# Feed-forward token groups of 384, 448 and 256, with one 512-column product for both halves of the last group

## The chip, the cores and the metric

One core of a Trainium2 chip runs the whole program. The metric is the device time of one launch in microseconds (us), as the median of three runs. TensorE (PE) does the matmuls, into eight PSUM banks of 512 fp32 columns; VectorE (DVE), ScalarE (ACT) and GpSimd (POOL) work elementwise; SyncE (SP) issues the DMAs. Each has its own instruction queue, and they wait for each other by semaphores.

## The reference

One inference step of one decoder layer, for 1024 prompt tokens and 8 x 8 sample tokens, 1088 in all, of width 1024:

```
def swiglu_ffn(x, g, w_gate, w_up, w_down):
    h = rmsnorm(x, g)
    return (jax.nn.silu(h @ w_gate) * (h @ w_up)) @ w_down

x = x + 0.5 * swiglu_ffn(x, ffn1...)                 # 1024 -> 2816 -> 1024
x = x + token_mixer(rmsnorm(x, mix_norm), ...)       # RG-LRU and GLA heads
x = x + cross_attend(x, mem_k, mem_v, ...)
x = x + 0.5 * swiglu_ffn(x, ffn2...)
y = rmsnorm(x, final_norm)
```

The change concerns the two feed-forward blocks, the norms before them and the final norm.

## The kernel before

The activations x lie in SBUF as [128, 8, 1088]: channels on partitions, 8 tiles of channels, tokens in the free dimension. Tokens go in three groups, `NS = [384, 384, 320]`; `tokens(n)` is the slice of group n. The same groups serve the feed-forward blocks and the mix.

**Products.** Every fp32 operand is split in a high part (rounded to the type fp32r) and a low part, the rest. `split_mm` (L1734 to L1738) makes a product of three matmuls: w_hi by x_hi, w_hi by x_lo, w_lo by x_hi, all accumulated in one PSUM bank.

**The feed-forward loop.** `ffn(f)` exists on each engine, for f = 0 and 1. It runs over 11 iterations of two tiles (ft) of the hidden width. The first and the last iteration are written out, nine run in a loop. An iteration on TensorE has six gate/up steps s, one for each ft and group n (in the first iteration the order is n slow, ft fast, so that both steps of group 2 come last; otherwise ft slow), each of 2 x 8 weight tiles, into banks 4 to 7 in two pairs (gate, up). Then come the down products: for each group n eight output tiles m, each of 2 weight tiles, into banks m % 4. Tile m waits until the addition three places back is done (`x_added`, the line `pe.wait_ge(x_added, ... + m - 3)`), so a bank is free again when TensorE returns to it.

**Behind a gate/up step**: ScalarE's silu from PSUM (L849); VectorE's product with the up bank (L1296, hf), its cast to h_hi (L1300) and the rest h_lo (L1302). **Behind a down tile**: VectorE adds half the bank to x (L1310). VectorE works strictly in order: the six steps' work, then the 24 additions.

**The weights**: per iteration SyncE loads six tiles of 512 KB each when the step that used the old ones is done (two after step 4 of 6, or 5 in the first iteration, two after step 6, two after the down products); ScalarE casts each (L772), GpSimd subtracts (L696). In the first feed-forward the same engines also split 60 tiles of the mix's weights for later (ScalarE L783, GpSimd L701).

**Norms** (rmsnorm) of a group: squares on ScalarE (L810), sums on VectorE (L1144, L1145) or GpSimd (L730, L732), column sums and spreading over the partitions by small matmuls (L1763, L1785), root on ScalarE (L823), scaling by VectorE (L1215, from x and a PSUM bank into frow), a_hi by ScalarE (L838), a_lo by VectorE (L1227). The norms of ffn groups 1 and 2 are made beside the first iteration's steps. In the last iteration of the first feed-forward VectorE makes the mix's first norm in between the additions of group 2; in the last of the second it makes rows of y (L1244) there, and then the remaining rows and their stores.

## Time and profile before

| | |
|---|---|
| median of 3 runs | 2378.79 us (2378.36 to 2382.55) |
| span of the profiled execution | 2379.0 us |
| TensorE busy | 2343.7 us, 99% |
| VectorE, ScalarE, GpSimd busy | 45%, 21%, 22% |
| TensorE's mean granted clock | 0.995 of full speed |
| first feed-forward, about | 8 to 811 us |
| mix and cross attention, about | 811 to 1568 us |
| second feed-forward and end, about | 1568 to 2379 us |
| a middle iteration of a feed-forward | 71.1 us |

The profile is of one execution; times in it are counted from the span's start. The recorded lengths of matmuls overlap, so what a matmul costs is read from the distance between starts. A bracket behind a row of the timeline gives the idle time of the engine before it and what ended it.

### The profile page before, as it was taken

How to read it: one execution, taken by the hardware profiler on the slowest of the kernel's cores; microseconds unless marked ns; L12 is line 12 of the kernel's file. 1: busy time of each engine (PE TensorE's matmuls, PEld its weight loads, DVE VectorE, ACT ScalarE, POOL GpSimd, SP SyncE). 2: the span in 40 equal slices, each digit the busy share in tenths (PEclk: the TensorE clock that was granted, in tenths of full speed). 3: DMA queues.
4: the chain of work that ended last, by engine and by line, in shares of the span. 5: the costliest groups of instructions: out<-in, count | busy, mean ns of one | idle time of the engine just before them, and what ended most of it. 6: DMA issues, size and time to landing. Idle time of an engine off the chain costs nothing. (4 is left out here: it accounts for less than half of the span.)

```text
span 2379.0 us, 36652 instructions
## 1 busy us (share of the span) xinstructions
PE 2343.7 (99%) x14996; PEld 2285.3 (96%) x14996; DVE 1062.5 (45%) x1696; ACT 494.6 (21%) x697; POOL 519.1 (22%) x239
## 2 busy tenths in 40 slices
PE   7999999999999999999999999999999999999998
PEld 7999999999999989899889999799999999999998
DVE  6434334444334574565642423444443344443345
ACT  4222212122211241321410221331111011111101
POOL 2444334344432000000001000022221222221121
PEclk9999999999999999999999999999999999999999
DMA  4554454454452465666678376731101010111112
GB/s 158 213 212 168 159 194 175 151 212 168 159 194 89 156 214 182 212 222 240 231 261 316 145 254 252 276 110 54 53 36 53 35 53 35 53 35 53 35 36 76
DMA packets 89475, 352.50 MB, mean 148 GB/s; under 512 B 8944, under 2 KB 16432, under 8 KB 79152
## 3 DMA queue, kind: packets, MB, share of 16 engines
q1 hardware_dynamic: 89104, 351.12, 40.3%
q8 instruction: 64, 1.05, 0.2%
q10 hardware_dynamic: 288, 0.18, 0.0%
q14 instruction: 19, 0.16, 0.0%
HBM read 280.54 MB, written 70.72 MB: 148 GB/s over the span
## 5 line engine op out<-in xcount | busy, mean ns | idle before, releaser
L1736 PE MATMUL ps<-a_hi,w_sb 128*128 128x384 f32 (+1 forms) x2112 | 691.6, 327 | 6.6 <-DVE a_lo L1227 4.6
L1738 PE MATMUL ps<-a_hi,w_sb 128*128 128x384 f32 (+1 forms) x2112 | 689.9, 327 | 0.0
L1737 PE MATMUL ps<-a_lo,w_sb 128*128 128x384 f32 (+1 forms) x2112 | 689.7, 327 | 0.0
L696 POOL TENSOR_TENSOR w_sb<-w_raw,w_sb 128x1024 fp32r<-128x1024 f32 x132 | 317.7, 2415 | 1066.4 <-ACT w_sb L772 1066.4
L1736 PEld LDWEIGHTS ps<-a_hi,w_sb 128*128 128x128 f32 x2112 | 397.7, 188 | 8.3 <-issue 3.5
L1737 PEld LDWEIGHTS ps<-a_lo,w_sb 128*128 128x128 f32 x2112 | 397.8, 188 | 0.0
L1738 PEld LDWEIGHTS ps<-a_hi,w_sb 128*128 128x128 f32 x2112 | 397.6, 188 | 0.0
L1310 DVE SCALAR_TENSOR_TENSOR x<-ps,x 128x384 f32<-128x384 f32 (+1 forms) x528 | 279.2, 534 | 199.7 <-PE ps L1738 199.7
L1296 DVE TENSOR_TENSOR hf<-sil,ps 128x384 f32<-128x384 f32 x132 | 70.1, 531 | 646.9 <-ACT sil L849 646.9
L1736 PE MATMUL ps<-h_hi,w_sb 128*128 128x384 f32 (+1 forms) x1056 | 344.7, 326 | 0.0
L1738 PE MATMUL ps<-h_hi,w_sb 128*128 128x384 f32 (+1 forms) x1056 | 344.2, 326 | 0.0
L1737 PE MATMUL ps<-h_lo,w_sb 128*128 128x384 f32 (+1 forms) x1056 | 344.1, 326 | 0.0
L849 ACT ACTIVATE sil<-ps 128x384 f32<-128x384 f32 x132 | 62.4, 473 | 1125.8 <-PE ps L1738 1125.7
L1302 DVE TENSOR_TENSOR h_lo<-hf,h_hi 128x384 fp32r<-128x384 f32 x132 | 239.5, 1815 | 4.6
L1736 PEld LDWEIGHTS ps<-h_hi,w_sb 128*128 128x128 f32 x1056 | 198.3, 188 | 0.3 <-DVE x L1310 0.3
L1737 PEld LDWEIGHTS ps<-h_lo,w_sb 128*128 128x128 f32 x1056 | 198.2, 188 | 0.0
L1738 PEld LDWEIGHTS ps<-h_hi,w_sb 128*128 128x128 f32 x1056 | 198.2, 188 | 0.0
L730 POOL TENSOR_TENSOR sq<-sq 128x768 f32<-128x768 f32 (+2 forms) x18 | 31.8, 1769 | 691.9 <-ACT sq L810 691.9
L772 ACT ACTIVATE w_sb<-w_raw 128x1024 fp32r<-128x1024 f32 x132 | 139.1, 1056 | 101.8 <-DMA w_raw<-in_ffn_gate 92.7
L701 POOL TENSOR_TENSOR st_w<-st_raw,st_w 128x1024 fp32r<-128x1024 f32 x60 | 145.2, 2448 | 48.8 <-ACT st_w L783 48.8
L1736 PE MATMUL ps<-mo_hi,w_sb 128*128 128x384 f32 (+1 forms) x384 | 125.7, 327 | 0.7 <-DVE mo_lo L1676 0.7
L1738 PE MATMUL ps<-mo_hi,w_sb 128*128 128x384 f32 (+1 forms) x384 | 125.1, 326 | 0.0
(262 smaller groups left out, 2717.2 us busy)
## 6 DMA issues: line engine op xcount, KB each, us to landing
w_sb<-split SPq DMA_DIRECT2D x148, 1024.0 KB, 5.2
split<-st_w SPq DMA_DIRECT2D x60, 1024.0 KB, 4.1
st_raw<-in_mix_tiles SPq DMA_DIRECT2D x60, 512.0 KB, 5.9
w_raw<-in_ffn_gate SPq DMA_DIRECT2D x44, 512.0 KB, 3.6
w_raw<-in_ffn_up SPq DMA_DIRECT2D x44, 512.0 KB, 4.4
w_raw<-in_ffn_down SPq DMA_DIRECT2D x44, 512.0 KB, 4.3
kc<-in_cache_k SPq DMA_DIRECT2D x5, 1024.0 KB, 8.5
kc<-in_cache_v SPq DMA_DIRECT2D x4, 1024.0 KB, 9.6
```

The source lines that it names most:

```text
L696: nc.gpsimd.tensor_tensor(w_lo_sb[:, slot_, :], raw[:, slot_, :], w_hi_sb[:, slot_, :].bitcast(F32), ALU.subtract)\
L701: nc.gpsimd.tensor_tensor(st_w[:, j % 3, 1, :], st_raw[:, j % 3, 1, :], st_w[:, j % 3, 0, :].bitcast(F32), ALU.subtract)\
L730: nc.gpsimd.tensor_tensor(buf[:, 0:2, 0:p.N], buf[:, 0:2, 0:p.N], buf[:, 2:4, 0:p.N], ALU.add).then_inc(pool_half, 1)
L772: nc.scalar.activation(w_hi_sb[:, slot_, :], raw[:, slot_, :], ACT.Copy).then_inc(w_hi, 1)
L849: nc.scalar.activation(sil[:, s % 2, 0:N], ps[:, 4 + 2 * (s % 2), 0:N], ACT.Silu).then_inc(silu_done, 1)
L1296: nc.vector.tensor_tensor(hf[:, s % 2, 0:N], sil[:, s % 2, 0:N], ps[:, b + 1, 0:N], ALU.mult).then_inc(h_done, 1)
L1302: nc.vector.tensor_tensor(h_lo[ft][:, tokens(n)], hf[:, s % 2, 0:N], h_hi[ft][:, tokens(n)].bitcast(F32), ALU.subtract)\
L1310: nc.vector.scalar_tensor_tensor(out=x[:, m, tokens(n)], in0=ps[:, m % 4, 0:NS[n]], scalar=0.5, in1=x[:, m, tokens(n)], op0=ALU.mult, op1= ...
L1736: nc.tensor.matmul(dst, w_h, x_h, start=start, stop=False)
L1737: nc.tensor.matmul(dst, w_h, x_l, start=False, stop=False)
L1738: return nc.tensor.matmul(dst, w_l, x_h, start=False, stop=stop)
```

## The change

1. The feed-forward blocks and the final norm get groups of their own: `FNS = [384, 448, 256]` at offsets 0, 384, 832 (`ftokens`). The mix keeps its groups. ffn2's norm of group 1 therefore also needs the first tokens of the last w_co group (`wait_source`), and VectorE's sum for it moves behind tile 6 of that stage (it was behind tile 4).
2. In group 2 (256 tokens) high and low halves lie in one tensor (`a_both`, `h_both`). `joint_mm` takes w_hi times both halves as one matmul of 512 columns, into both halves of a bank, and w_lo times the high half as one of 256 into the first half. The two halves of the bank are still to be summed.
3. For that, behind a gate/up step of group 2 ScalarE copies the second halves of both banks (`part`), VectorE sums them with the first (`whole`), and silu and product read `whole`, in SBUF. Behind the down tiles of group 2 VectorE adds two tiles (two banks) at once: first half of both, then second half of both, the second instruction waiting for the first (`add_pair`).
4. Buffers move to make room.

```diff
+            def joint_mm(dst, w_h, w_l, x_both, start, stop):
+                N = x_both.shape[2]
+                nc.tensor.matmul(dst[:, 0:2 * N].rearrange("p (a n) -> p a n", a=2), w_h, x_both, start=start, stop=False)
+                return nc.tensor.matmul(dst[:, 0:N], w_l, x_both[:, 0], start=False, stop=stop)
...
+                                if n == 2:
+                                    ins = joint_mm(ps[:, b, :], w_hi_sb[:, w, c], w_lo_sb[:, w, c], a_both[:, :, k, :], k == 0, k == KT - 1)
+                                else:
+                                    ins = split_mm(ps[:, b, 0:FNS[n]], w_hi_sb[:, w, c], w_lo_sb[:, w, c],
+                                                   a_hi[n][:, k, :], a_lo[n][:, k, :], k == 0, k == KT - 1)
...
+                                if n == 2:
+                                    ins = joint_mm(ps[:, m % 4, :], w_hi_sb[:, 4 + ft, c], w_lo_sb[:, 4 + ft, c],
+                                                   h_both[ft][:, :, ftokens(2)], ft == 0, ft == 1)
...
-                    nc.scalar.activation(sil[:, s % 2, 0:N], ps[:, 4 + 2 * (s % 2), 0:N], ACT.Silu).then_inc(silu_done, 1)
+                    N = FNS[n]
+                    b = 4 + 2 * (s % 2)
+                    if n == 2:
+                        ft, _ = ffn_step(first, s)
+                        nc.scalar.activation(part[:, :, :], ps[:, b:b + 2, N:2 * N], ACT.Copy).then_inc(part_out, 1)
+                        act.wait_ge(whole_out, f * 2 * ITS + q0 // 6 * 2 + ft + 1)
+                        nc.scalar.activation(sil[:, s % 2, 0:N], whole[:, 0, :], ACT.Silu).then_inc(silu_done, 1)
...
+                        if n == 2:
+                            dve.wait_ge(part_out, f * 2 * ITS + 2 * it + ft + 1)
+                            nc.vector.tensor_tensor(whole[:, :, :], part[:, :, :], ps[:, b:b + 2, 0:N], ALU.add).then_inc(whole_out, 1)
...
-                        nc.vector.tensor_tensor(hf[:, s % 2, 0:N], sil[:, s % 2, 0:N], ps[:, b + 1, 0:N], ALU.mult).then_inc(h_done, 1)
+                        up = whole[:, 1, :] if n == 2 else ps[:, b + 1, 0:N]
+                        nc.vector.tensor_tensor(hf[:, s % 2, 0:N], sil[:, s % 2, 0:N], up, ALU.mult).then_inc(h_done, 1)
...
+                        def add_pair(m):
+                            d = X + Q * it + KT * n + m
+                            N = FNS[n]
+                            rows = x[:, m:m + 2, ftokens(n)]
+                            dve.wait_ge(down_done, d + 2)
+                            if f or not first:
+                                dve.wait_ge(x_added, d - Q + 2)
+                            nc.vector.scalar_tensor_tensor(out=rows, in0=ps[:, m % 4:m % 4 + 2, 0:N], scalar=0.5,
+                                                           in1=rows, op0=ALU.mult, op1=ALU.add).then_inc(x_half_added, 1)
+                            dve.wait_ge(x_half_added, f * 4 * ITS + 4 * it + m // 2 + 1)
+                            nc.vector.scalar_tensor_tensor(out=rows, in0=ps[:, m % 4:m % 4 + 2, N:2 * N], scalar=0.5,
+                                                           in1=rows, op0=ALU.mult, op1=ALU.add).then_inc(x_added, 2)
...
-                                add(2 * i)
-                                add(2 * i + 1)
+                                add_pair(2 * i)
...
-                            for m in range(KT):
-                                fin_rows(0, m, m + 1)
-                                add(m)
+                            for m in range(0, KT, 2):
+                                fin_rows(0, m, m + 2)
+                                add_pair(m)
...
-                eng.wait_ge(evicted, FIRST["co", n] + 8)
+                eng.wait_ge(evicted, FIRST["co", min(n + 1, 2) if n else 0] + (4 if n == 1 else 8))
...
-                    if n == 2 and j == 4:
+                    if n == 2 and j == 6:
                         norm_sum("ffn2", 1, 0)
```

## Rows read from the trace of the kernel before

**Rows 1.** The page's first part: busy us (share of the span) xinstructions of each engine.

```profile
PE 2343.7 (99%) x14996; PEld 2285.3 (96%) x14996; DVE 1062.5 (45%) x1696; ACT 494.6 (21%) x697; POOL 519.1 (22%) x239
```

**Rows 2.** Groups by shape, PE: shapes xcount, busy us, mean ns, idle before.

```profile
L1736 PE MATMUL ps<-a_hi,w_sb 128*128 128x384 f32 x1408 | 473.9, 337 | 5.4 <-DVE a_lo L1227 3.3 <-POOL w_sb L696 1.4 <-DVE x L1378 0.6
```

**Rows 3.** Timeline of PE, a middle iteration: start us, us, instruction.

```profile
1899.80 0.33 PE L1736 MATMUL ps<-a_hi,w_sb 128*128 128x384 f32 x1
...
1902.92 0.31 PE L1736 MATMUL ps<-a_hi,w_sb 128*128 128x320 f32 x1
...
1909.95 0.34 PE L1736 MATMUL ps<-h_hi,w_sb 128*128 128x384 f32 x1
```

**Rows 4.** Timeline of PE in two other stages: 256 and 512 columns.

```profile
1189.79 0.28 PE L1737 MATMUL ps<-xm_lo,w_sb 128*128 128x256 f32 x1
...
1191.35 0.28 PE L1738 MATMUL ps<-xm_hi,w_sb 128*128 128x256 f32 x1
...
1239.75 0.39 PE L1900 MATMUL ps<-w_sb,xm_hi 128*128 128x512 f32 x1
...
1242.93 0.39 PE L1902 MATMUL ps<-w_sb,xm_hi 128*128 128x512 f32 x1
```

**Rows 5.** Groups by shape, DVE and ACT.

```profile
L1310 DVE SCALAR_TENSOR_TENSOR x<-ps,x 128x384 f32<-128x384 f32 x352 | 193.2, 556 | 139.0 <-PE ps L1738 139.0
...
L1645 DVE TENSOR_TENSOR mo_lo<-ps,mo_hi 128x512 fp32r<-128x512 f32 x16 | 10.9, 690 | 17.9 <-ACT mo_hi L1052 17.8
```

**Rows 6.** Timelines of PE and DVE: a tile's last matmul, its addition.

```profile
1927.34 0.31 PE L1738 MATMUL ps<-h_hi,w_sb 128*128 128x320 f32 x1
...
1927.78 0.49 DVE L1310 SCALAR_TENSOR_TENSOR x<-ps,x 128x320 f32<-128x320 f32 x1 [0.40 <-PE ps L1738]
```

**Rows 7.** Timeline of PE: the one wait for an addition.

```profile
808.44 0.42 PE L1736 MATMUL ps<-h_hi,w_sb 128*128 128x320 f32 x1
808.70 0.32 PE L1737 MATMUL ps<-h_lo,w_sb 128*128 128x320 f32 x1
```

**Rows 8.** Timelines of ACT, DVE, POOL after step 5 (its last matmul starts 1909.80).

```profile
1910.15 0.44 ACT L849 ACTIVATE sil<-ps 128x320 f32<-128x320 f32 x1 [5.59 <-PE ps L1738]
...
1911.57 0.49 DVE L1302 TENSOR_TENSOR h_lo<-hf,h_hi 128x320 fp32r<-128x320 f32 x1
1911.98 1.01 DVE L1310 SCALAR_TENSOR_TENSOR x<-ps,x 128x384 f32<-128x384 f32 x2
...
1915.12 4.75 POOL L696 TENSOR_TENSOR w_sb<-w_raw,w_sb 128x1024 fp32r<-128x1024 f32 x2 [8.08 <-ACT w_sb L772]
```

**Rows 9.** Timelines of POOL, DVE, PE in the first iterations.

```profile
71.22 4.77 POOL L696 TENSOR_TENSOR w_sb<-w_raw,w_sb 128x1024 fp32r<-128x1024 f32 x2 [2.22 <-ACT w_sb L772]
...
74.36 1.82 DVE L1300 CAST h_hi<-hf 128x320 fp32r<-128x320 f32 x1
...
1613.11 0.41 PE L1736 MATMUL ps<-a_hi,w_sb 128*128 128x320 f32 x1 [0.64 <-DVE a_lo L1227]
```

**Rows 10.** Timeline of DVE, last iteration of the first feed-forward.

```profile
805.99 1.13 DVE L1215 SCALAR_TENSOR_TENSOR sq<-x,vec,ps 128x384 f32<-128x384 f32 x2
807.03 0.95 DVE L1227 TENSOR_TENSOR xn_lo<-sq,xn_hi 128x768 fp32r<-128x768 f32 x1
807.90 0.88 DVE L1310 SCALAR_TENSOR_TENSOR x<-ps,x 128x320 f32<-128x320 f32 x2
808.70 1.13 DVE L1215 SCALAR_TENSOR_TENSOR sq<-x,vec,ps 128x384 f32<-128x384 f32 x2
```

**Rows 11.** Timeline of DVE, last iteration of the second feed-forward.

```profile
2356.46 0.61 DVE L1244 SCALAR_TENSOR_TENSOR yb<-x,vec,ps 128x384 f32<-128x384 f32 x1 [1.03 <-PE ps L1785]
...
2357.39 0.60 DVE L1244 SCALAR_TENSOR_TENSOR yb<-x,vec,ps 128x384 f32<-128x384 f32 x1
```

**Rows 12.** Timeline of ACT at the start.

```profile
14.72 1.48 ACT L810 ACTIVATE sq<-x 128x1536 f32<-128x1536 f32 x1 [1.84 <-DMA x<-in_x]
```

More of the change, by code:

```diff
@@ L35 @@
 NMAX = 384
+FOFFS = [0, 384, 832]
+FNS = [384, 448, 256]
+FMAX = 448
 NPROMPT = [384, 384, 256]
@@ L270, in program @@
         x, o = at("x", [P, KT, TOK], base)
-        sq, o = at("sq", [P, 4, NMAX], o)
+        part, q = at("part", [P, 2, FNS[2]], o)
+        whole, _ = at("whole", [P, 2, FNS[2]], q)
+        sq, o = at("sq", [P, 4, FMAX], o)
         cst, o = at("cst", [P, NC_A], o)
@@ L286, in program @@
         yb, q = at("yb", [P, KT, TOK], operands)
-        sq_c, q = at("sq_c", [P, 4, NMAX], q)
-        sq_d, _ = at("sq_d", [P, 4, NMAX], q)
+        sq_c, q = at("sq_c", [P, 4, FNS[2]], q)
+        sq_d, _ = at("sq_d", [P, 4, FNS[2]], q)
         a_hi, a_lo = [None] * 3, [None] * 3
-        for n in range(3):
-            a_hi[n], o = at(f"a_hi{n}", [P, KT, NS[n]], o, F32R)
-            a_lo[n], o = at(f"a_lo{n}", [P, KT, NS[n]], o, F32R)
+        for n in range(2):
+            a_hi[n], o = at(f"a_hi{n}", [P, KT, FNS[n]], o, F32R)
+            a_lo[n], o = at(f"a_lo{n}", [P, KT, FNS[n]], o, F32R)
+        a_both, o = at("a_both", [P, 2, KT, FNS[2]], o, F32R)
+        a_hi[2], a_lo[2] = a_both[:, 0], a_both[:, 1]
         h_hi, h_lo = [None] * 2, [None] * 2
         frow, _ = at("frow", [P, 4, TOK], o)
+        h_both = [None] * 2
         for i in range(2):
-            h_hi[i], o = at(f"h_hi{i}", [P, TOK], o, F32R)
-            h_lo[i], o = at(f"h_lo{i}", [P, TOK], o, F32R)
-        sil, o = at("sil", [P, 2, NMAX], o)
-        sq_b, _ = at("sq_b", [P, 4, NMAX], o - 4 * 2 * NMAX)
-        hf, o = at("hf", [P, 2, NMAX], o)
+            h_both[i], o = at(f"h_both{i}", [P, 2, TOK], o, F32R)
+            h_hi[i], h_lo[i] = h_both[i][:, 0], h_both[i][:, 1]
+        sil, o = at("sil", [P, 2, FMAX], o)
+        sq_b, _ = at("sq_b", [P, 4, FMAX], o - 4 * 2 * FMAX)
+        hf, o = at("hf", [P, 2, FMAX], o)
         slot = 4096
@@ L476, in tokens, with ftokens, group @@
             return slice(OFFS[n], OFFS[n] + NS[n])
+        def ftokens(n):
+            return slice(FOFFS[n], FOFFS[n] + FNS[n])
+        def group(kind, n):
+            return ftokens(n) if kind in ("ffn1", "ffn2", "fin") else tokens(n)
         def norm_source(kind, n, q):
@@ L484, in norm_source @@
                 return osb[:, :, 0:N]
[L485 removed]
+            return (memx if kind == "mem" else x)[:, 4 * q:4 * q + 4, slice(0, N) if kind == "mem" else group(kind, n)]
         GATE_UP_STEPS = 6 * ITS
@@ L677, in store_y @@
             def store_y(n, rows):
-                sp.dma_start(out["y"].rearrange("(k p) t -> p k t", p=P)[:, rows, tokens(n)], yb[:, rows, tokens(n)]).then_inc(y_stored, 16)
+                sp.dma_start(out["y"].rearrange("(k p) t -> p k t", p=P)[:, rows, ftokens(n)], yb[:, rows, ftokens(n)]).then_inc(y_stored, 16)
             for n in range(3):
@@ L792, in norm_squares @@
                         wait_source(act, kind, n)
+                    elif (kind, n) == ("ffn2", 1):
+                        act.wait_ge(evicted, FIRST["co", 2] + 8)
                     if q == 0:
```

52 lines of the change are left out of this document (28 added, 24 removed).

## The prediction

> **What bounds the kernel now.** I read the page's busy shares first: TensorE is busy for 2343.7 of 2379.0 us, VectorE for 45% [rows 1]. The groups by line and shape say with what: the largest are the feed-forward products, three matmuls per weight tile [rows 2]; by the code they are 9504 matmuls, and 22 iterations of 71.1 us are two thirds of the span. The timeline of TensorE in a middle iteration then shows neither a gap between tiles nor between token groups: 18 matmuls of 384 columns take 3.12 us, 173.3 ns each, and the 48 of 320 behind them take 7.03 us, 146.5 ns each [rows 3]. So only two things can move the time: what TensorE must issue, and new waits of TensorE. VectorE, ScalarE and GpSimd have slack, but each piece of it has a deadline, and the second half of this working goes through the deadlines.
>
> **The products.** 384 columns at 2.4 GHz are 160.0 ns, 320 are 133.3: every matmul costs 13.3 ns beyond its columns. The other sizes that the change uses follow the same law in other stages: 13 steps of 256 columns take 1.56 us (120.0 ns, again 13.3 over), 14 of 512 take 3.18 us (227 ns, 13.8 over) [rows 4]. Columns stay the same: 3x(384+384+320) = 3264 before, 3x384 + 3x448 + 512 + 256 = 3264 after. Matmuls go from 9 to 8 per weight tile; 48 weight tiles (32 gate/up, 16 down) in 22 iterations make 1056 fewer, x 13.3 ns = -14.1 us, or -0.64 an iteration (gate/up 2 x -0.21, down -0.21; inside down group 1 is 1.28 us longer, group 2 1.49 shorter). I take the moving operand with two halves far apart at the price of a plain one; no row shows such a one, so its bounds are 0 and the whole gain.
>
> The Trainium skill ("TensorE: Matmul & The Clock Gate", Back-to-back issue gap) gives N/2.4 + 2.5 ns when warm. By it the same removal would be worth 2.6 us, and the forecast 11.5 us later. The rows above show 13.3 ns at four sizes, so they decide.
>
> **The new wait: additions by pairs.** In group 2 of the down products a tile is now 2 x (226.7+120.0) = 0.693 us. Four PSUM banks rotate, so tile 4 needs tile 0 added. Before, one addition (0.56 us at 384 columns) was ready long before. Now tiles 0 and 1 are added together, after tile 1, by two instructions of 512 elements, the second waiting for the first. A 512-element VectorE operation from PSUM takes 0.690 us [rows 5]. From the start of a tile's last matmul to the start of its addition pass 0.44 us [rows 6], about 0.42 with 256 columns. When an addition is late, its end to the next matmul is 0.05 us (the first of the two at 807.90 ends at about 808.39, and TensorE goes on at 808.44), and the restart costs another 0.10: 0.26 us to the second matmul in place of 0.147 [rows 7, 10]. Counted from group 2's first matmul: last matmul of tile 1 at 1.27, additions 1.69 to 2.38 and 2.41 to 3.10, tile 4 at 3.15 where it was due at 2.77. Stall 0.38 + 0.10 = 0.48 to 0.49 us. The second pair ends at 4.52, before tile 6 is due at about 4.65: no second stall. In 20 iterations (all but the last of either feed-forward): +9.8 us (bounds 8 and 12, for 0.1 us in the hand-over). That eats two thirds of the gain.
>
> **The joint step's chain.** Before, silu starts 0.35 us after the step's last matmul starts, and the first addition of group 0, queued behind h_lo on VectorE, at +2.18 us; TensorE needs it by +4.28 (four tiles of 1.04) [rows 8]. The new order is: copy of 512 (0.60) and sum of 512 (0.69) [rows 5], then silu 0.41, product 0.43, h_hi 0.30 and h_lo 0.43, taken down from 320 to 256 columns at about 1 ns a column on VectorE (320 take 0.49 [rows 8]) and 0.8 on ScalarE, with hand-overs of 0.03 to 0.10: first addition from +3.34 to +3.90, TensorE served at +3.95. Cost 0, but the cover falls from 1.5 us to 0.33. GpSimd is idle there: its next subtraction starts at 1915.12, 5.3 us after that last matmul [rows 8]. This matters since the product now reads SBUF alone, and such VectorE work waits for GpSimd: h_hi, some 0.3 us, took 1.82 at 74.36 under GpSimd's 71.22 to 75.99, ending 0.19 after it [rows 9]. The Trainium skill ("SBUF — State Buffer") says that the shared port pair is locked for the whole instruction and that an operation with a PSUM input keeps out of it; the trace agrees with both, by this row and by additions that stay at 0.56 under GpSimd.
>
> **First iterations** (both joint steps come one after the other, at the end). Gain: TensorE's wait of about 0.99 us (1612.34 due, 1613.11 served, plus restart and a second, smaller one) for group 2's normalisation goes, as group 1 gives 2.6 us more cover: -0.99 twice [rows 9]. Loss: the last step's chain meets GpSimd's two subtractions of the next iteration's weights. In the first feed-forward step 5 ends at 71.9 on the old time scale, the copy waits for ScalarE's two casts until 73.5, the product waits for GpSimd until 76.9, the first addition ends at 78.7, TensorE was due at 76.1: +2.75 (bounds 0 and 7, for one subtraction more or less). In the second the same reckoning gives 1629.95 against 1628.4: +1.65. The sums of squares of group 1 at 448 columns add 0.5 in the second and 0.2 in the first (up to 1.6 if a sum of 0.95 us, which starts just ahead of a subtraction, falls behind it). Together +3.1.
>
> **Last iterations.** VectorE sets the pace there already. In the first feed-forward its cycle per two tiles is scale, low part, two additions: 805.99 to 808.70, 2.71 us, of which the additions are 0.80 [rows 10]. The two dependent ones of 512 take 1.33 to the next start, so the cycle is 3.24. Tile 4 is served at 4.26 and tile 6 at 7.50 (due 3.55 and 5.75); the mix's first tile, which needs the last low part, ends 17.3 us after group 2's old start in place of 14.1. Against a pure product gain that is +3.4. In the second, a row of y and an addition take 0.93 a tile [rows 11]; two rows and a pair now take 2.37, so the last addition is 3.2 us later; the y rows behind it are as long as before (8 x 0.60 + 8 x 0.41 against 8.0), and so is the store. +3.2.
>
> **The start.** ScalarE takes group 1's squares at 14.72, when its x lands, ahead of the casts that group 0 needs [rows 12]. 448 columns are 256 KB more at about 390 GB/s, +0.66, and 0.2 more of squaring: +0.9.
>
> Sum: -14.1 + 9.8 + 3.1 + 3.4 + 3.2 + 0.9 = +6.3 us. The profiled span is 2379.0, the median of the runs 2378.8, so the sum goes on either unchanged: 2385.1. Things that I cost at nothing: the later squares of ffn2's group 1 (they run in the last w_co tiles, where ScalarE is idle), the moved buffers, single additions of 448 columns (0.62 us against tiles of 1.2).
>
> **Rivals.**
> (a) No stall at tile 4: the pair would be in before 2.77 us, which decides at 1.03 us for both additions from their start. For it: VectorE overlaps neighbouring instructions by 0.08. Against: here one waits for the other, and 2 x 0.69 is 1.38. Gives 2385.1 - 9.8 = 2375.3; this is the side on which the kernel is not slower.
> (b) The joint step's chain passes its 0.33 us. One GpSimd subtraction over it blocks for up to 2.4 us, so 2.0 us in the ten iterations of one feed-forward: 2405. For it: in the first feed-forward GpSimd and the queue are fuller. Against: the subtractions hang on weight loads that are only issued when this step ends.
> (c) The joint product saves nothing, because its two halves lie apart or its weight loads don't hide: 2385.1 + 14.1 = 2399.2. Against it: the 120.0 and 227 ns [rows 4].
> With the 2.5 ns that the Trainium skill gives (the section named above) the time would be 2385.1 + 11.5 = 2396.6; I count that under this rival.
>
> **How the numbers follow.** Forecast 0.60, with an own range of 2381 to 2389; (a) 0.22; (b) 0.11; (c) 0.07. Half of (a), about 0.10, lies below 2374.0, which is 0.2% (about what a measurement of this kernel tells from no change). Between there and 2383.6 lie the rest of (a) and a third of the forecast: 0.31. Above: 0.59. The range takes in most of (a) and, above, the forecast's own tail with the larger bound of the first iterations: 2374.5 to 2392.
>
> **What would show it.** The matmul pitch in group 2 must be 227 and 120 ns, the iteration 71.0 us where it was 71.1. Each iteration must show one wait of TensorE for x in group 2, at tile 4, of some 0.4 us, and none at tile 4 of group 0. The last iterations must show two waits, at tiles 4 and 6, the first iterations one of 1.5 to 3 us at tile 4 of group 0. If TensorE has no wait for a pair, I am wrong towards (a); if h_lo of the joint step grows beyond 0.5 us in middle iterations, towards (b).

## The result and the profile after

The changed kernel takes 2412.7 us (median; 2411.7 to 2416.5) where the kernel before takes 2380.7 beside it: ratio 1.014, 95% interval [1.0125, 1.0154]. The forecast was 2385.1, the range ended at 2392. The slowdown was forecast, at a fifth of its size: the profiled span is 2409.9 us, 30.9 longer than before, where the sum gave 6.3. The question of this study is where the other 24.6 us are.

The page of after, first part (busy us and share, xinstructions), to be held against [rows 1]:

```profile
PE 2357.8 (98%) x13940; PEld 2188.6 (91%) x13940; DVE 1138.3 (47%) x1740; ACT 522.2 (22%) x741; POOL 520.0 (22%) x239
```

1056 matmuls are gone, as planned, and TensorE is still busy for all of the span, but for 14.1 us more than before. A few waits more can't be read from this; that the matmuls themselves have become dearer can. The timeline of TensorE in a middle iteration of after shows it (start us, length us, engine, line, operation). Down products of group 0, then group 1, then the first of group 2:

```profile
221.40 0.34 PE L1781 MATMUL ps<-h_both,w_sb 128*128 128x384 f32 x1
...
229.72 0.36 PE L1781 MATMUL ps<-h_both,w_sb 128*128 128x448 f32 x1
...
239.64 0.40 PE L1788 MATMUL ps<-h_both,w_sb 128*128 128x512 f32 x1
```

48 matmuls of 384 columns take 8.32 us, 173.3 ns each, as in [rows 3]. The 48 of 448 columns take 9.92 us: 206.6 ns each. By the law of the prediction, N/2.4 + 13.3 ns, they should take 200.0. An iteration has 144 such matmuls and there are 22: 144 x 22 x 6.6 ns = 20.8 us.

The joint products do what was hoped. TensorE and VectorE in group 2 of the same iteration, at its tile 4:

```profile
241.38 0.39 PE L1788 MATMUL ps<-h_both,w_sb 128*128 128x512 f32 x1
241.60 0.28 PE L1789 MATMUL ps<-h_both,w_sb 128*128 128x256 f32 x1
241.72 0.39 PE L1788 MATMUL ps<-h_both,w_sb 128*128 128x512 f32 x1
...
242.30 0.28 PE L1789 MATMUL ps<-h_both,w_sb 128*128 128x256 f32 x1
242.86 0.50 PE L1788 MATMUL ps<-h_both,w_sb 128*128 128x512 f32 x1 [0.28 <-DVE x L1353]
243.20 0.28 PE L1789 MATMUL ps<-h_both,w_sb 128*128 128x256 f32 x1
```

```profile
241.32 0.69 DVE L1350 SCALAR_TENSOR_TENSOR x<-ps,x 128x512 f32<-128x512 f32 x1 [0.86 <-PE ps L1789]
242.11 0.69 DVE L1353 SCALAR_TENSOR_TENSOR x<-ps,x 128x512 f32<-128x512 f32 x1
```

512 and 256 columns together take 0.34 to 0.35 us, the 227 and 120 ns of [rows 4]. The forecast wait for the pair is there: from 242.30 to 242.86 pass 0.56 us instead of 0.12, and the next step 0.34 instead of 0.23. That is 0.55 us an iteration against the 0.49 of the prediction; the second addition starts 0.10 us after the first has ended, where 0.03 was taken. Tile 6 doesn't wait, as forecast.

The joint step's chain on ScalarE and VectorE (step 5, before group 0's additions):

```profile
221.60 0.60 ACT L871 ACTIVATE part<-ps 128x512 f32<-128x512 f32 x1 [4.06 <-PE ps L1789]
222.96 0.42 ACT L873 ACTIVATE sil<-whole 128x256 f32<-128x256 f32 x1 [0.76 <-DVE whole L1321]
```

```profile
223.41 0.43 DVE L1326 TENSOR_TENSOR hf<-sil,whole 128x256 f32<-128x256 f32 x1 [0.48 <-ACT sil L873]
223.94 0.29 DVE L1330 CAST h_both<-hf 128x256 fp32r<-128x256 f32 x1
224.27 0.43 DVE L1332 TENSOR_TENSOR h_both<-hf,h_both 128x256 fp32r<-128x256 f32 x1
224.61 1.94 DVE L1340 SCALAR_TENSOR_TENSOR x<-ps,x 128x384 f32<-128x384 f32 x4
```

The first addition starts 3.3 us after the step's last matmul, the +3.34 of the prediction, and TensorE has no wait in group 0: the copy and the sum cost nothing here.

In the first iteration they do cost. TensorE of after at step 5 and at tile 4 of group 0:

```profile
67.35 0.28 PE L1789 MATMUL ps<-a_both,w_sb 128*128 128x256 f32 x1
68.17 0.50 PE L1788 MATMUL ps<-a_both,w_sb 128*128 128x512 f32 x1 [0.54 <-DVE hf L1326]
...
77.95 0.34 PE L1783 MATMUL ps<-h_both,w_sb 128*128 128x384 f32 x1
80.03 0.44 PE L1781 MATMUL ps<-h_both,w_sb 128*128 128x384 f32 x1 [1.74 <-DVE x L1340]
...
81.36 0.52 PE L1781 MATMUL ps<-h_both,w_sb 128*128 128x384 f32 x1
81.68 0.52 PE L1782 MATMUL ps<-h_both,w_sb 128*128 128x384 f32 x1
```

The 0.8 us at 67.35 were not in the sum. The wait at 77.95 was, at 2.75; it is 2.0. Behind it ten matmuls come 0.32 us apart: the windows of that stretch (us, busy us and instructions of PE, PEld, DVE, ACT and POOL, granted clock, DMA share, GB/s) show the clock below full after the pause.

```profile
73.00:77.00 4.00, 4.00 (x25) 3.86 (x24) 2.08 (x5) 2.50 (x4) 3.39 (x2) 1.00 1.02 430
80.50:84.00 3.50, 3.50 (x14) 3.48 (x14) 1.91 (x4) 0.00 (x0) 0.00 (x0) 0.57 1.01 364
```

Eleven matmuls take 3.41 us where 1.9 would do, +1.5. This does not follow the pause each time. One of the later runs, the one with operands moved by 16 and 16 columns, has the same pause, from 77.95 to 80.07, and in its window 23 matmuls in place of 14 and the full clock:

```profile
80.50:84.00 3.50, 3.50 (x23) 3.50 (x22) 2.53 (x5) 0.00 (x0) 0.00 (x0) 1.00 1.01 357
```

Of the 18 traces in which TensorE's starts are 1.8 to 2.2 us apart at that place, five show the lower clock behind it. In the second feed-forward that wait costs 1.75 (forecast 1.65). The last iteration of the first feed-forward, whose cycle on VectorE was 2.71 us in [rows 10]:

```profile
820.30 0.28 PE L1789 MATMUL ps<-h_both,w_sb 128*128 128x256 f32 x1
821.21 0.50 PE L1788 MATMUL ps<-h_both,w_sb 128*128 128x512 f32 x1 [0.63 <-DVE x L1353]
...
822.61 0.28 PE L1789 MATMUL ps<-h_both,w_sb 128*128 128x256 f32 x1
824.53 0.50 PE L1788 MATMUL ps<-h_both,w_sb 128*128 128x512 f32 x1 [1.65 <-DVE x L1353]
```

Its two waits, at tiles 4 and 6, are the ones forecast; the cycle is 3.32 us against 3.24.

### The profile page after: what moved, and what is told of

The parts are those of the page before. It is cut to its first block and busy times, and to the rows that moved or that the text cites. A ratio compares the mean times of both kernels' runs of the same rounds, so it can differ in the third digit from the quotient of the medians.

```text
span 2409.9 us, 34705 instructions
## 1 busy us (share of the span) xinstructions
PE 2357.8 (98%) x13940; PEld 2188.6 (91%) x13940; DVE 1138.3 (47%) x1740; ACT 522.2 (22%) x741; POOL 520.0 (22%) x239
## 5 line engine op out<-in xcount | busy, mean ns | idle before, releaser
L1781 PE MATMUL ps<-a_hi,w_sb 128*128 128x448 f32 (+1 forms) x1408 | 497.5, 353 | 6.5 <-DVE a_lo L1253 4.1
L1782 PE MATMUL ps<-a_lo,w_sb 128*128 128x448 f32 (+1 forms) x1408 | 495.7, 352 | 0.0
L1783 PE MATMUL ps<-a_hi,w_sb 128*128 128x448 f32 (+1 forms) x1408 | 495.6, 352 | 0.0
L1781 PEld LDWEIGHTS ps<-a_hi,w_sb 128*128 128x128 f32 x1408 | 265.5, 189 | 21.8 <-issue 4.4
L1783 PEld LDWEIGHTS ps<-a_hi,w_sb 128*128 128x128 f32 x1408 | 265.4, 189 | 12.9
L1782 PEld LDWEIGHTS ps<-a_lo,w_sb 128*128 128x128 f32 x1408 | 265.7, 189 | 12.2
L1781 PE MATMUL ps<-h_both,w_sb 128*128 128x384 f32 (+1 forms) x704 | 248.2, 353 | 3.2 <-DVE x L1340 3.2
L1783 PE MATMUL ps<-h_both,w_sb 128*128 128x384 f32 (+1 forms) x704 | 247.8, 352 | 0.0
L1782 PE MATMUL ps<-h_both,w_sb 128*128 128x384 f32 (+1 forms) x704 | 247.7, 352 | 0.0
L1788 PE MATMUL ps<-a_both,w_sb 128*128 128x512 f32 x704 | 246.4, 392 | 0.5 <-DVE hf L1326 0.5
L1332 DVE TENSOR_TENSOR h_both<-hf,h_both 128x384 fp32r<-128x384 f32 (+1 forms) x132 | 237.2, 1797 | 4.5
L1789 PE MATMUL ps<-a_both,w_sb 128*128 128x256 f32 x704 | 197.1, 280 | 0.0
L1788 PEld LDWEIGHTS ps<-a_both,w_sb 128*128 128x128 f32 x704 | 131.7, 187 | 29.1 <-DVE hf L1326 0.9
L1781 PEld LDWEIGHTS ps<-h_both,w_sb 128*128 128x128 f32 x704 | 132.7, 189 | 10.9 <-DVE x L1340 3.9
L1783 PEld LDWEIGHTS ps<-h_both,w_sb 128*128 128x128 f32 x704 | 132.6, 188 | 6.5
```

Of the source, the lines that this page charges most:

```text
L1332: nc.vector.tensor_tensor(h_lo[ft][:, ftokens(n)], hf[:, s % 2, 0:N], h_hi[ft][:, ftokens(n)].bitcast(F32), ALU.subtract)\
L1781: nc.tensor.matmul(dst, w_h, x_h, start=start, stop=False)
L1782: nc.tensor.matmul(dst, w_h, x_l, start=False, stop=False)
L1783: return nc.tensor.matmul(dst, w_l, x_h, start=False, stop=stop)
L1788: nc.tensor.matmul(dst[:, 0:2 * N].rearrange("p (a n) -> p a n", a=2), w_h, x_both, start=start, stop=False)
L1789: return nc.tensor.matmul(dst[:, 0:N], w_l, x_both[:, 0], start=False, stop=stop)
```

## The experiments

Two theories to begin with. (1) Size: a matmul of 448 columns costs 206.6 ns by itself. (2) Neighbourhood: the joint products, their buffers or their additions slow the others.

**Eight sizes, eight places.** Group 1's down tiles m = 0 to 7 take other sizes (first run) or read from and write to other columns (second).

```diff
-  split_mm(ps[:, m % 4, 0:FNS[n]], ..., h_hi[ft][:, ftokens(n)], h_lo[ft][:, ftokens(n)], ...)
+  _, to, N = PLACES[m] if n == 1 else (FOFFS[n], 0, FNS[n])   # a start, a bank column, a size for each m
+  split_mm(ps[:, m % 4, to:to + N], ..., h_hi[ft][:, at_:at_ + N], h_lo[ft][:, at_:at_ + N], ...)
```

The waits for the hidden layer and the additions are adapted to that.

> The changed kernel, but the eight down tiles of group 1 take 400, 416, 432, 440, 456, 464, 480 and 496 columns in place of 448, all from token 384 on (part of the sums is left out, or columns too many are computed). It asks where the 206.7 ns of a 448-column matmul come from, 6.7 more than columns at 2.4 GHz plus 13.3. Theory of the size: the surcharge belongs to certain column counts, wherever they lie; then some of the eight stand on the line (180.0, 186.7, 193.3, 196.7, 203.3, 206.7, 213.3, 220.0 ns) and others 3 to 7 ns above it. Rival, the place: what starts at token 384, or has these strides, costs 6.7 ns more; then all eight stand 6.7 above the line.

> The changed kernel, but the eight down tiles of group 1 take: 448 columns from token 384, from 383, from 320, from 0; 448 from 384 into the bank from column 64 on; 446, 384 and 512 columns from 384 (so group 1's sums are taken from other tokens, or from fewer or more of them). Theory of the size: the first five all cost 206.7 ns, the last two 173.3 and 226.7. Rival, the place: the pitch changes with the start (200.0 from 320 or 0), or with the place in the bank, and 384 and 512 columns from token 384 cost 180.0 and 233.3.

Mean distance of starts in the six matmuls of a tile, with N/2.4 + 13.3 ns in brackets. First run: 400 columns 180.0 (180.0), 416 187.4 (186.7), 432 197.9 (193.3), 440 199.5 (196.7), 456 208.9 (203.3), 464 209.7 (206.7), 480 216.8 (213.3), 496 224.7 ns (220.0). Second run, 448 columns: from column 384 205.7, from 383 200.9, from 320 205.7, from 0 206.7, into bank column 64 206.7; 446 columns 200.9 (199.2), 384 173.3 (173.3), 512 231.5 (226.7). So the law holds up to 400 columns and breaks above, unevenly. The one start that stands out, 383, was read at first as "odd starts are better".

**The groups alone, more banks, the joint product for gate/up alone.** Three changes to the kernel after.

```diff
# groups alone: no joint product, no part and whole, single additions; groups 384, 448, 256 stay
-  if n == 2:
+  if False:
# two more banks: the joint down tiles in banks 0 1 2 3 6 7 0 1, TensorE's waits moved accordingly
+  def down_bank(m, last):
+      return m % 4 if last else (0, 1, 2, 3, 6, 7, 0, 1)[m]
# gate/up alone: down products of group 2 as split_mm with single additions
```

> Groups of 384, 448 and 256, but three matmuls per weight tile in every group and additions one by one, as before. Theory of the size: 144 matmuls of 448 columns in each of 22 iterations cost 6.7 ns more each, 21.1 us in all, and with 0.9 at the start and some 0.7 in the second feed-forward's first norms the time is 2401 to 2404 us. Rival, the joint products (their weight loads or their split operand disturb the 448-column matmuls beside them): the pitch of 448 columns falls to 200 ns and the time is 2379 to 2383.

> The changed kernel, but in all iterations but the last of either feed-forward the down tiles 4 and 5 of group 2 go to banks 6 and 7, and 6 and 7 to banks 0 and 1, so tile 4 needn't wait for the first pair. Theory, the pair's wait costs what it shows (20 times 0.55 us): the wait at tile 4 disappears and the time falls by 11 us, to about 2401.7. Rival, it comes back as a wait at tile 6 or at the next iteration's step 1: the time stays within 3 us of 2412.7.

> The changed kernel with joint products in gate/up alone; the down products of group 2 are three matmuls with single additions, as before. Against the changed kernel's 2412.7: 352 matmuls come back (+4.7 us), the pair's wait goes (20 times 0.55, -11.0), the last iterations are VectorE-bound as before the change (-6.6). Theory: 2399.8, within 2. Rival, the last iterations are late because of the longer group 1 and not because of the pairs: 2406.

Measured: groups alone 2403.9 us (ratio 1.0103 [1.0086, 1.012]), 448 columns still at 206.6 ns. That is 24 us above before with nothing joint in it, and theory 2 falls. Two more banks: 2400.0 (1.0084 [1.0067, 1.0101]), 12.8 us under after; no wait is left in its middle iterations. Gate/up alone: 2398.8 (1.0076 [1.0059, 1.0093]). A middle iteration is 71.97 us long in after, 71.36 with more banks and 71.57 with the joint product in gate/up alone: the joint down product saves 0.21 us an iteration and its wait costs 0.61, so in the middle iterations the wait alone makes it a loss, of 0.4. With the wait gone the whole kernel is still no faster than without joint down products (2400.0 against 2398.8), mainly since the pairs of the last iterations remain (3.6 us, by the last runs below).

**Starts.** Is it odd starts? Tiles of 448 columns from 382, 381, 380, 376, 385, three other sizes from 383, and a_hi of group 1 one column later.

> The changed kernel, but the eight down tiles of group 1 take 448 columns from 382, 381, 380, 376 and 385, then 512, 456 and 432 columns from 383 (sums over other tokens). In the run of places 448 columns from 383 cost 200.6 ns, from 384, 320 and 0 206.1 to 206.7. And a_hi of group 1 lies 4 bytes further in SBUF, a_lo does not. Theory of the odd start (an operand that begins 4 bytes off an 8-byte border escapes the surcharge): 381 and 385 cost 200.0, the even ones 206.7; 512, 456 and 432 from 383 cost 226.7, 203.3 and 193.3; in gate/up the matmuls of a_hi cost 200.0 and that of a_lo 206.7. Rival, 383 was chance of another kind (the tile before or behind it, or the rhythm with the weight loads): odd and even starts cost the same, and a_hi like a_lo.

448 columns: from 382 205.8 to 206.7, 381 206.7, 380 200.0 to 200.7, 376 202.5 to 203.3, 385 206.5 ns. From 383: 512 227.7 to 227.9, 456 202.8 to 203.0, 432 193.3, all three within 1.2 ns of their lines. The gate/up matmuls of a_hi took 207.3 and 205.8, those of a_lo 203.4.

The edit moved more than it says. `at` rounds every offset up to 32 bytes, so the 4 bytes more in group 1's a_hi put all that lies behind it, a_lo, group 2's halves and the hidden layer, 8 columns further on. In the kernel after's own count the five tiles start at 390, 389, 388, 384 and 393, the other three at 391, and a_lo at +8. The tile from 376 therefore reads the very places that group 1's down products read in after, and takes 1.22 us for six matmuls where they take 1.24:

```profile
233.28 0.36 PE L1789 MATMUL ps<-h_both,w_sb 128*128 128x448 f32 x1
...
234.50 0.37 PE L1789 MATMUL ps<-h_both,w_sb 128*128 128x448 f32 x1
```

Odd and even decide nothing, but the start does matter. The tile from 376 says that it isn't all: same place, same size, but 202.5 to 203.3 in place of 206.7 ns between other neighbours. With rows of six a start can't be told from its neighbours, and I turned to sizes instead, which proved the wrong turn.

**Smaller groups.** 416 had been near its line. Groups of 416, 416 and 256, first with all else of after, then with the two more banks and, in the last iterations, single additions; and a profiled execution on pairs of matmuls. (Beyond the sizes, the larger group 0 gets a place of its own for its halves in the second feed-forward, and that block's first norm waits for more of w_co; so it is in the runs with 408 and 424 too.)

```diff
-FOFFS = [0, 384, 832]
-FNS = [384, 448, 256]
+FOFFS = [0, 416, 832]
+FNS = [416, 416, 256]
```

> Groups of 416, 416 and 256 tokens, with the joint products and the additions by pairs as in the kernel after. No matmul is above 416 columns, the last size that lay on N/2.4 + 13.3 ns when sizes were tried one by one (416: 186.7 ns). The same two groups then cost 2 x 186.7 = 373.4 ns for each pair of matmuls, against 173.3 + 206.7 = 380.0 in the kernel after: 6.67 ns x 144 x 22 = 21.1 us less, 2412.7 - 21.1 = 2391.6 us (2389 to 2394), if the surcharge is a matter of the size of one matmul. Rival: 448 columns is slow because of what the larger group does elsewhere (the longer hidden-layer steps, the uneven split); then some of it stays, and the time lies between 2395 and 2412. Second rival: 416 columns is on the line only beside groups of another size; then the pitch of both groups is above 186.7 and the time above 2394.

> Groups of 416, 416 and 256 tokens, two more banks for the joint down products (as in the run with two more banks, which was worth 12.8 us), and in the last iterations group 2's down products of three matmuls with single additions again. Terms from the measured time after, 2412.7: surcharge -21.1, pair waits of the middle iterations -12.8, the waits of the two last iterations (3.4 and 3.2 predicted, 3.6 and 1.5 seen) -5: 2373.8 us (2371 to 2378), about 0.3% under the kernel before (2379 to 2381). Rival: the wait that the added banks take away comes back at the gate/up products, because groups of 416 in place of 384 make step 0's additions end later: then 2380 or more.

> One look at what the surcharge above 416 columns goes with. Seven of the eight down tiles of group 1 are changed (their sums are not the reference's): six matmuls each, tile 1 reads the high halves of the hidden layer for all of them, tile 2 uses the high halves of the weights for all, tile 3 both, tiles 4 to 7 alternate 448 with 384 columns, take 384 for every third, alternate 448 with 416, and alternate 480 with 448. If a matmul above 416 is slow by itself, the mean of tile 4 is (206.7 + 173.3)/2 = 190.0 ns, of tile 6 (206.7 + 186.7)/2 = 196.7. If only the second of two such in a row is slow (the first 448 after a 384 was at 201), tile 4 has 186.7 and tile 6 193.3. If the surcharge comes from which operand moves, tile 1 or tile 3 is at 200.0; if from a change of the weights, tile 2 or tile 3 is at 200.0; if from neither, all three are at 206.7.

2409.5 us (1.0117 [1.0101, 1.0132]) where 2391.6 was expected, and 2390.0 (1.0041 [1.0027, 1.0055]) with banks. The timeline of the first, its down products of groups 0 and 1:

```profile
222.31 0.35 PE L1788 MATMUL ps<-h_both,w_sb 128*128 128x416 f32 x1
...
231.35 0.35 PE L1788 MATMUL ps<-h_both,w_sb 128*128 128x416 f32 x1
...
240.47 0.39 PE L1795 MATMUL ps<-h_both,w_sb 128*128 128x512 f32 x1
```

48 of the same size take 9.04 us (188.3 ns) from column 0 and 9.12 (190.0) from column 416. Same size, same line of code, other start, other time: the second hint at the start. The pairs: with the same moving tensor, the same weights or both, still 206.7 ns; 448 alternating with 384 gave 201 and 179 (mean 191.0), with 416 196.8. The mean is that of two matmuls that each carry their surcharge, but part of the 448's appears in the 384 behind it.

**Sizes in longer rows**, and the best pair from it. The gate/up products of all iterations but the first take eight sizes, 24 matmuls in a row each.

> One look at the pitch of matmuls of one size, 24 in a row, for eight sizes: in all iterations but the first the gate/up products of group 0 take 400, 408, 424 and 432 columns and those of group 1 take 512, 440, 464 and 480 (the columns beyond the group's own go to bank columns that nobody reads, and 440 leaves 8 tokens of one product out, so the sums are not the reference's). The run of 416-column groups gave 189.8 ns in long rows, where 416 among other sizes had given 187.4, so a size has to be measured in a row. If the surcharge depends on the size alone, the values of the run with eight sizes come again: 400 at 180.0, 432 at 197.9, 440 at 199.5, 464 at 209.7, 480 at 216.8, each within 0.5 ns. If it needs a row of the same size, they are higher, by up to 7 ns. For 512 columns the mixing stage shows 227 and the run with starts 231.5 beside 448s: 226.7 would make groups of 320 and 512 tokens the cheapest pair for the joint product (146.7 + 226.7 = 373.4 ns against 380.0), 231.5 would not.

> The version with two more banks and single additions in the last iterations (2390.0 us with groups of 416, 416 and 256), now with 408, 424 and 256 tokens. In rows of 24 the sizes one by one gave 184.9 ns for 408 columns and 190.1 for 424, together 375.0, against 2 x 189.75 = 379.5 for two groups of 416. 144 x 22 x 4.5 ns = 14.3 us less: 2375.7 us (2373 to 2379), 0.2% under the kernel before (2380.8). Rival: in longer rows (96 of one size in place of 24) the pitch creeps up again, as 416 did from 187.4 in six to 189.75; then the time stays near 2385 or above.

> The kernel after with nothing changed but the group sizes, 408, 424 and 256 for 384, 448 and 256. If the time above the forecast is the surcharge of the sizes, 380.0 - 375.0 = 5.0 ns x 144 x 22 = 15.8 us go: 2412.7 - 15.8 = 2396.9 us (2394 to 2400), while groups of 416 gained 3.2. Rival as for the run beside it: the pitch of long rows is higher, and the time between 2400 and 2410.

Means of 24, the line in brackets: 400 180.7 (180.0), 408 184.9 (183.3), 424 190.1 (190.0), 432 195.8 (193.3), 440 199.8 (196.7), 464 209.0 (206.7), 480 216.7 (213.3), 512 228.1 ns (226.7). Of all sizes tried, 448 at its place has the largest surcharge. But 408 and 424 as groups gave 2391.6 us with banks (1.0047 [1.0033, 1.0061]) and 2409.0 without (1.0118 [1.0102, 1.0133]), not 2375.7 and 2396.9: in the down products the 424 from column 408 stood at 193.6 ns, in gate/up at 192.6, against 190.1 in the rows of 24, and 408 in gate/up at 185.8 against 184.9. A size has no price of its own above 400 columns. Both forecasts failed by the same step as the first one: a price taken at one place and used at another.

**The start, in rows of 24.** All gate/up matmuls of groups 0 and 1 take 448 columns; the rows differ only in where the moving operand starts.

```diff
+STARTS = [(0, 60, 56, 32), (63, 16, 48, 60)]      # the second run: (4, 8, 24, 40), (62, 61, 12, 2)
-  a_hi[n][:, k, :], a_lo[n][:, k, :]
+  wide(n, 0, k, 448, STARTS[n][w]), wide(n, 1, k, 448, STARTS[n][w])   # 448 columns from that start
```

> One look: in all iterations but the first every gate/up product of groups 0 and 1 takes 448 columns, in eight rows of 24 matmuls that differ in the column where the moving rows start, counted from the multiple of 64 columns at which the kernel after has them: 0, 60, 56, 32 for group 0's rows (384 columns apart) and 63, 16, 48, 60 for group 1's (448 apart). Columns that aren't the group's own go into the sums, so these are not the reference's. If the surcharge of 448 columns hangs on where the read starts, 0 is at 206.7 ns, 60 and 63 near 200 to 201 (as 380 and 383 were in rows of six), 56 at 203, and the two rows at 60 agree. If it was the neighbours in those rows of six, all eight are at 206 to 207. A place at 200 in a row of 24 would let the kernel after keep its groups and lose the 21 us.

> The same look with eight other starts: 4, 8, 24, 40 for group 0's rows and 62, 61, 12, 2 for group 1's. By the rows of six, 62 and 61 are at 206 to 207 although 60 and 63 were not; if a start decides, they are so again and 4 to 40 show what the good ones have in common (a multiple of four columns that is none of eight would put 4, 12 and 60 at 200 and 8, 24, 40 at 203 to 207). If starts decide nothing, all are at 206 to 207.

Timeline of the first of the two, a row from start 16 between its neighbours (24 matmuls):

```profile
115.18 0.36 PE L1789 MATMUL ps<-a_hi,w_sb 128*128 128x448 f32 x1
...
119.98 0.39 PE L1796 MATMUL ps<-a_hi,w_sb 128*128 128x512 f32 x1
```

4.80 us, 200.0 ns each: on the line. The means over 20 iterations, by start in columns from a multiple of 64 (counted from the first column of the normalised halves):

| start | ns | start | ns | start | ns |
|---|---|---|---|---|---|
| 0 | 205.8 | 16 | 200.0 | 56 | 204.6 |
| 2 | 205.5 | 24 | 205.2 | 60 | 202.5 and 202.8 |
| 4 | 202.0 | 32 | 203.6 | 61 | 207.8 |
| 8 | 203.7 | 40 | 200.5 | 62 | 202.8 |
| 12 | 203.0 | 48 | 202.3 | 63 | 201.2 |

The start is worth up to 8 ns, with no order that I can see (multiples of four columns are at 200 as well as at 205). The expectation for 61 and 62 rested on the starts of the run before as they were written, not as they lay. Start 60 gave the same in rows 384 and 448 columns apart. There is a memory in it too: the row from start 8 took 200.0, 204.4 or 206.0 ns in different iterations, the same instructions on the same places.

**The kernel after, moved.** If this is the cause, moving operands must give back the 21 us with no instruction changed. The hidden layer's halves (down products) move by 64 bytes. To make room, the normalised halves of groups 1 and 2 change places, by 16 and 28 KB, and group 1's move 64 bytes on top; in the rows of 24, 64 bytes alone had given 200.0. The weights stay where they were.

```diff
+A1, H_SHIFT = 16, 16          # columns; the run beside it: 16, 252
+a_both, h_place = at("a_both", [P, 2, KT, FNS[2]], o, F32R)          # ahead of group 1's halves now
+a_one, o = at("a_one", [P, 2 * KT * FNS[1] + A1], h_place, F32R)    # group 1's halves, A1 columns later
+h_both[i] = h_all[:, extra + 2 * TOK * i:extra + 2 * TOK * (i + 1)]...  # H_SHIFT columns later in all
```

> The kernel after with the same work and the same sizes; only its places in SBUF differ: group 1's normalised halves start 16 columns (64 bytes) later, where a row of 24 matmuls of 448 columns took 200.0 ns, and the hidden layer's halves 252 columns later, which puts group 1's part 4 columns ahead of a multiple of 256 as 380 was in rows of six (200.0 to 200.7). If the start of the moving rows decides, the 96 gate/up matmuls of group 1 in an iteration are at 200.0 and the 48 down matmuls at 200 to 202: up to 21 us less, 2392 to 2396 us (gate/up alone: 13.5 us, 2399). If the starts in those looks helped only beside their neighbours, 206.7 stays and with it 2412.7.

> As the run beside it, but the hidden layer's halves are moved by 16 columns (64 bytes), like the normalised ones. Gate/up again at 200.0 (same place as beside it). If what counts is the 64 bytes against the kernel after, whatever tensor is read, the down matmuls are at 200.0 too and the time is 2392; if the place that is good for one tensor says nothing of the other, they are anywhere from 200 to 207, the time 2392 to 2399.

With 16 and 16: 2393.0 us, ratio 1.0057 [1.0041, 1.0074], 19.7 us under after. With 16 and 252: 2403.8, 1.0095 [1.0078, 1.0112]. The timeline of the first, down products of group 1 and, further on, its gate/up products:

```profile
226.72 0.36 PE L1788 MATMUL ps<-h_all,w_sb 128*128 128x448 f32 x1
...
236.32 0.39 PE L1795 MATMUL ps<-h_all,w_sb 128*128 128x512 f32 x1
...
250.82 0.36 PE L1788 MATMUL ps<-a_one,w_sb 128*128 128x448 f32 x1
...
260.42 0.39 PE L1795 MATMUL ps<-a_both,w_sb 128*128 128x512 f32 x1
```

Twice 48 matmuls in 9.60 us: 200.0 ns, both. The iteration is 71.25 us long where after has 71.97: 0.72 x 22 = 15.8 of the 19.7 us; the stretch at half clock, which this run doesn't have at 81 us, is 1.5 more, and one in the second feed-forward's first iteration, which both have, is shorter here by 1.3. Whether these two come with the places or with the two executions is not shown; 15.8 us, net, is what the matmuls have given. The gain would be 4.2 us larger (3 ns x 64 x 22), but the joint gate/up products, at 173.5 ns a matmul in after, now stand at 176.5. In the two runs with rows of 24 these products had kept their place, and they stood at 176.5 too, except behind the row from start 60, where they had 173.8: what runs ahead of them can do this with their own place unchanged. In the run with 16 and 16 both changed. The run with 252 differs from it in the place of the hidden layer alone. It was meant to repeat the good 380 of the rows of six, but by the 8 columns above that was 388, and 252 puts group 1's part at 60 from a multiple of 64 instead. Its timeline:

```profile
219.35 0.34 PE L1788 MATMUL ps<-h_all,w_sb 128*128 128x384 f32 x1
...
227.97 0.37 PE L1788 MATMUL ps<-h_all,w_sb 128*128 128x448 f32 x1
...
237.72 0.40 PE L1795 MATMUL ps<-h_all,w_sb 128*128 128x512 f32 x1
```

9.75 us, 203.1 ns, for 448 columns, and 8.62 us, 179.6 ns, for 384: this place makes even the size slow that stood at 173.3 to 174.8 everywhere else. Nothing else that TensorE reads differs between the two runs, and the place is worth 10.8 us (2403.8 against 2393.0).

Counted from a multiple of 64 columns, the hidden layer's starts agree with the rows of the table, which read another tensor: 16 at 200.0 and 200.0, 60 at 202 to 203 and 202.5 to 202.8, 63 at 200.9 and 201.2, 4 (written as 380) at 200.7 and 202.0, 0 at 206.7 and 205.8. The exception is the one tile from 0 with 202.5 to 203.3, above.

**All together.** Places moved, two more banks, single additions in the last iterations; and the same with group 2's halves moved too.

```diff
+A1, H_SHIFT = 16, 16
+return m % 4 if last else (0, 1, 2, 3, 6, 7, 0, 1)[m]
-if n == 2:
+if n == 2 and not last:
# the run beside it, in addition:
-a_both, h_place = at("a_both", [P, 2, KT, FNS[2]], o, F32R)
+a_both, h_place = at("a_both", [P, 2, KT, FNS[2]], o + 64, F32R)
```

> The sum of what the runs found: groups of 384, 448 and 256 tokens, places as in the run with 16 and 16 columns (2393.0 us), two more banks for the joint down products (-12.8) and, in the last iterations, three matmuls and single additions for group 2 again (-5): 2375.2 us (2372 to 2379), 0.2% under the kernel before (2380.5), ratio 0.998. The joint gate/up products, which stood at 176.5 ns a matmul in that run against 173.5 in the kernel after, stay there. Rival: taking the waits away shifts the rows against each other and a part of the surcharge comes back in the down products; then 2380 to 2390.

> As the run beside it, with group 2's normalised halves moved by 16 columns too, so that all of the moving rows but group 0's lie 64 bytes later than in the kernel after. If the joint gate/up products went to 176.5 ns because only they had stayed in place, they are at 173.5 again: 3.0 ns x 64 x 22 = 4.2 us less than beside it, 2371 us (2368 to 2375), ratio 0.996. If each tensor has its own good place, anything from 173.5 to 180 can come and the time is within 5 us of the run beside it, on either side.

2381.2 us, ratio 1.000 [0.9991, 1.001], and 2382.9, 1.0006 [0.9996, 1.0015]: level with before, not 0.2% under it. Moving group 2's halves left their products at 176.4 ns; that fits what runs ahead of them as the cause, but doesn't show it, since one other place is no more than one try. Between the run with 16 and 16 and the first of these the timelines give: 20 middle iterations of 70.67 us in place of 71.25, -11.7 (forecast -12.8); the last iterations, from group 2's first matmul to the mix's first tile 8.8 us in place of 11.3 and to the end 26.6 in place of 27.6, -3.6 (forecast -5); but the first two iterations 1.9 us longer than that, where a stretch at half clock is back, and the mixing stage 0.9 longer. Against before, a middle iteration is 0.4 us shorter, some 8 us in all, and the start, the first iterations and VectorE's work in the last ones take them back. None of the versions beats the kernel before.

## Why the prediction was wrong, point by point

The signs were right, the mechanisms that were named are all in the trace, and one term was set to zero that was the largest. The spans, us over before (one profiled execution of each):

| term | forecast | trace |
|---|---|---|
| 1056 fewer matmuls | -14.1 | -14.1 |
| 448-column matmuls above N/2.4 + 13.3 ns | 0 | +20.8 |
| pair additions, 20 waits | +9.8 | +11.0 |
| first iterations | +3.1 | +4.2 |
| last iteration, first feed-forward | +3.4 | +3.8 |
| last iteration, second feed-forward | +3.2 | +4.6 |
| start | +0.9 | +0.8 |
| sum | +6.3 | +31.1 (span: +30.9) |

*The products.* The step that failed is the one that took a law from sizes of 256, 320, 384 and 512 columns and applied it to 448 between them; 200.0 ns never stood in a row of the trace. It had 3168 matmuls behind it, so that an error of 3% in the price is 21 us, three times the room that the range had above the forecast. The prediction gave bounds for the moving operand with two halves, which turned out as taken, and none for the size that had no row at all. The runs show 206.6 ns to be a matter of place for the most part: with the hidden layer 64 bytes further on the same down products take 200.0, with it 252 columns further on 203.1, and nothing else that TensorE reads differs between those two runs. What runs ahead has a share that no run measured by itself. That the four sizes of the rows agreed was less evidence than it looked, since up to 400 columns places rarely show (173.3 to 174.8 ns at all but one), and 512 columns stood at 231.5 in another place. The excess of 13.3 ns itself held, at 384, at 512 with 256 and, at a good place, at 448.

*The pair's wait* was right in place and number and 0.06 us short, because the dependent addition starts 0.10 us after the one before it, not 0.03. Rival (a), no wait, is out; the run with more banks shows that the waits are worth 12.8 us, where the timeline of after has 11.0 in the middle iterations.

*The joint step's chain* (rival b) was right to 0.04 us. *The joint product* (rival c) saves what was said.

*The first iterations.* In the second feed-forward the wait came as reckoned (1.75 us against 1.65). In the first I missed that VectorE's late product also holds up step 5, by 0.8 us; the wait itself was 0.7 shorter than said. The pause was followed by a stretch at half clock in this execution, +1.5, which was in no sum and comes in some executions and not in others. The statistics' small matmuls of the larger group take 0.4 us more in the first, those of the smaller group 2 0.7 less, which the sum left out. From start to start, less the first three rows of the table, the first iteration is 3.4 us longer than before and that of the second feed-forward 0.8.

*The last iterations.* Right mechanism, cycle 3.32 against 3.24. The second one was sized 1.4 too small: counted from group 2's first down matmul, 0.8 of it up to the end of the last addition and 0.7 behind it. The rows of y behind it were forecast rightly, 8.02 us for the sixteen in both kernels; but the first of them waits 1.0 us for TensorE's norm matmuls where it waited 0.2. The terms add up to the span within 0.2 us.

Rival (b) had the time nearest to the result, 2405, by a mechanism that isn't there; no rival had the right one, a dearer matmul.

## What to carry to other kernels

When a change gives a matmul a size that no row of the trace shows, its price needs bounds like any other unknown, times the number of matmuls; agreement at neighbouring sizes is no substitute. Above 400 columns of fp32r, compare distances of starts for each tensor and group at once after the change, and try other places in SBUF before anything is rebuilt: here 16 columns were worth 0.8% for no instruction. Note the starts as they lie after rounding, not as they are written. A place must be tried in the kernel itself, because what runs ahead counts too. And two dependent instructions on the way to a PSUM bank cost more than the matmul they save, unless the banks allow one tile more of distance.

## What the runs showed of the hardware

The time of a matmul with a moving operand of more than 400 fp32r columns depends in these runs on where in SBUF that operand starts: 200.0 to 207.8 ns for 448 columns, 188.3 and 190.0 for 416 in the same kernel, and once 179.6 instead of 173.3 for 384. Starts that agree modulo 64 columns gave times within 1.3 ns of each other in two tensors, in five cases of six. The bank column written, a change of the moving tensor and a change of the weights did not matter where they were tried. Part of it is history: one row had three values in different iterations, the joint gate/up products took 173.5 or 176.5 ns at one place, and a surcharge can show in the matmul behind. The Trainium skill ("SBUF — State Buffer", Operand start alignment) says that an operand may start at any multiple of its element size and adds that this is about legality and not about speed; all starts tried here were legal by it, and the speed is what differed. What in the chip does this stays open. The recorded weight loads are 187 to 188 ns long and start 2 to 3 ns behind their matmul; that is about the length at which the surcharge begins (400 columns are at 180.0 ns, 416 at 186.7 by the line), which would fit a contention between the two reads, but that is an idea: no run separated them.

After a pause of 1.9 us between stretches of full load, ten matmuls ran at 320 ns where 173 is usual: the granted clock of that stretch is 0.57, its lower level of 1.2 GHz for part of it. In 13 of the 18 traces with such a pause the clock stayed at its full level of 2.4 GHz. Of two additions on VectorE, 512 columns from PSUM each, the one that waits for the other starts 0.10 us after its end; TensorE's second matmul after a wait comes 0.10 us late.
